# A two-layer RWKV and pooling trunk on one core: the row pitch of the FFN's input and the place of the residual's scalings

## The reference

```python
x = _layer_norm(ALPHA * x + h, ln_g[i, 0], ln_b[i, 0])
h = x @ w_in
gate, up = h[..., :D_FF], h[..., D_FF:]
x = _layer_norm(ALPHA * x + (jax.nn.silu(gate) * up) @ w_down, ln_g[i, 1], ln_b[i, 1])
```

## Time and profile before

| | |
|---|---|
| median of 3 runs | 2718.19 us (2717.26 to 2719.93) |
| profiled execution, its own time | 2718.26 us |
| its span, first to last instruction | 2716.7 us |
| TensorE matmuls, busy share of the span | 96% |
| VectorE, ScalarE, GpSimd | 64%, 43%, 5% |
| mean granted clock of TensorE, share of full speed | 0.982 |

### The profile page before, as it was taken

One profiled execution on the slowest core, in us unless ns is written; L12 is line 12 of the kernel. 1 busy time (PEld: TensorE's weight loads), 2 busy tenths in 40 slices (PEclk: granted clock), 3 DMA queues, 4 the chain that ended last, 5 costly groups with the idle time before them and its releaser, 6 DMA issues.

```text
span 2716.7 us, 56956 instructions
## 1 busy us (share of the span) xinstructions
PE 2595.1 (96%) x23305; PEld 2494.3 (92%) x23305; DVE 1744.5 (64%) x2764; ACT 1160.1 (43%) x1782; POOL 140.6 (5%) x211
## 2 busy tenths in 40 slices
PE   7979999999998899999999999878999999999997
PEld 7978888888788899999999999878999999999997
DVE  7877888888857655654455554686556444655546
ACT  5565555555534433333333333444333333333334
POOL 0000111111101000000000000100000000000000
PEclk9989999999999999999999999989999999999999
DMA  7622222222346556546665556524555556555553
GB/s 212 180 81 74 76 83 77 83 83 83 100 113 194 144 155 169 161 139 169 183 167 157 162 140 169 164 82 124 156 163 157 149 163 188 162 162 157 145 163 96
DMA packets 707053, 379.35 MB, mean 140 GB/s; under 512 B 16023, under 2 KB 699191, under 8 KB 706711
## 3 DMA queue, kind: packets, MB, share of 16 engines
q1 hardware_dynamic: 701040, 363.46, 47.8%
q0 software_dynamic: 5792, 13.34, 1.8%
q10 hardware_dynamic: 70, 0.39, 0.1%
HBM read 367.31 MB, written 10.62 MB: 139 GB/s over the span
## 4 chain that ended last, share of the span: by engine, by line
PE 80%; DVE 12%; ACT 4%; issue 2%; DMA 1%; DVEq 0%; SPq 0%; ACTq 0%
PE PS L741 24%; PE PS L742 23%; PE PS L743 23%; PE PS L894 3%; DVE WL L1739 3%; ACT WH L1270 2%; DVE PL L1856 1%; DVE ML L1754 1%; DVE TM L1747 1%; PE PS L926 1%; PE PS L1013 1%; PE PS L963 0%; PE PS L968 0%; PE PS L931 0%; DVE X L2214 0%
## 5 line engine op out<-in xcount | busy, mean ns | idle before, releaser
L1739 DVE TENSOR_TENSOR WL<-RAW,WH 128x2048 fp32r<-128x2048 f32 (+1 forms) x325 | 658.9, 2028 | 604.4 <-ACT WH L1270 604.3
L741 PE MATMUL PS<-UH,WH 128*128 128x290 f32 x2784 | 832.1, 299 | 17.0 <-DVE WL L1739 16.4
L1270 ACT ACTIVATE WH<-RAW 128x2048 fp32r<-128x2048 f32 (+1 forms) x325 | 552.0, 1699 | 648.1 <-PE PS L743 644.7
L743 PE MATMUL PS<-UH,WL 128*128 128x290 f32 x2784 | 827.2, 297 | 0.0
L742 PE MATMUL PS<-UL,WH 128*128 128x290 f32 x2784 | 824.7, 296 | 0.0
L741 PEld LDWEIGHTS PS<-UH,WH 128*128 128x128 f32 x2784 | 527.3, 189 | 18.9 <-issue 18.8
L742 PEld LDWEIGHTS PS<-UL,WH 128*128 128x128 f32 x2784 | 530.0, 190 | 0.1
L743 PEld LDWEIGHTS PS<-UH,WL 128*128 128x128 f32 x2784 | 525.7, 189 | 0.0
L741 PE MATMUL PS<-HH,WH 128*128 128x288 f32 x1408 | 413.9, 294 | 3.3 <-DVE WL L1739 3.3
L742 PE MATMUL PS<-HL,WH 128*128 128x288 f32 x1408 | 415.3, 295 | 0.0
L743 PE MATMUL PS<-HH,WL 128*128 128x288 f32 x1408 | 415.0, 295 | 0.0
(11 more groups left out here) (328 smaller groups left out, 3483.8 us busy)
## 6 DMA issues: line engine op xcount, KB each, us to landing
RAW<-in_ffn_w_in SPq DMA_DIRECT2D x176, 1024.0 KB, 5.7
RAW<-in_ffn_w_down SPq DMA_DIRECT2D x128, 704.0 KB, 4.8
RAW<-in_rw_wr SPq DMA_DIRECT2D x16, 1024.0 KB, 6.7
PR<-in_rw_wk SPq DMA_DIRECT2D x64, 256.0 KB, 3.0
PR<-in_rw_wv SPq DMA_DIRECT2D x64, 256.0 KB, 2.9
PR<-in_rw_wo SPq DMA_DIRECT2D x64, 256.0 KB, 3.2
S0N<-in_state_wkv POOLq DMA_DIRECT2D x64, 64.0 KB, 2.3
out<-SOS POOLq DMA_DIRECT2D x64, 64.0 KB, 2.7
```

The lines of the kernel that those rows point to most:

```text
L741: pe.matmul(out, wh, xh, start=first, stop=False)
L743: return pe.matmul(out, wl, xh, start=False, stop=last)
L1270: act.activation(WH[0:rows, j % 2, 0:n], RAW[0:rows, j, 0:n], ACT.Copy).then_inc(hi_ready, 1)
L1739: dve.tensor_tensor(WL[0:rows, j % 2, 0:n], RAW[0:rows, j, 0:n], WH[0:rows, j % 2, 0:n].bitcast(F32), ALU.subtract).then_inc(lo_ready, 1)
```

## The change

UH and UL get rows of 320 columns, 1280 bytes apart, of which 290 are used. They take 40,960 bytes up to the start of MH1: from the region's start UH is at 97,728 and UL at 118,208, both multiples of 64 and 64 more than multiples of 256. For it, ML0 follows MH0 without the 128 bytes between, and SUM and C12 move to XPS, NLN and GATE to LHH, LIN behind DP. UL's block c is kept in row (c + 2) mod 16. With these places 10 blocks, not 12, are free while the last units run (EARLY_IN). `gains_lo` writes in two pieces where its blocks go round the end. `scaled` and `normed` take a start block and do 4 blocks; they are called after each of the first four hidden units of a layer, for which the second call of `up` is written out too.

```diff
+EARLY_IN = 10
...
-        ML[0] = at("ML0", [P, KC, T], F32R, after("MH0") + 128)
+        ML[0] = at("ML0", [P, KC, T], F32R, after("MH0"))
...
-        UH = at("UH", [P, KC, T + 2], F32R, place["MH0"][0] - 128)
-        UL = at("UL", [P, KC, T + 2], F32R, place["ML0"][0] - 128)
...
+        UH = at("UH", [P, KC, 320], F32R, place["MH1"][0] - 2 * KC * 1280)
+        UL = at("UL", [P, KC, 320], F32R, after("UH"))
+        SUM = at("SUM", [P, T], F32, place["XPS"][0])
...
+        def ul(c):
+
+            return (c + 2) % KC
...
-                                     UH[:, k, :], UL[:, k, :], k == 0, k == KC - 1)
+                                     UH[:, k, 0:T + 2], UL[:, ul(k), 0:T + 2], k == 0, k == KC - 1)
...
-                        if kind == "late" and m < 12:
+                        if kind == "late" and m < EARLY_IN:
...
-            gains_hi(0, 12, KC)
-            for c in range(12, KC):
+            gains_hi(0, EARLY_IN, KC)
+            for c in range(EARLY_IN, KC):
                 input_hi(0, c)
...
+                for a, b in ((a, min(b, KC - 2)), (KC - 2, b)):
+                    for at, col in ((T, PCOL["ln_g"]), (T + 1, PCOL["ln_b"])):
+                        if a < b:
+                            dve.tensor_tensor(UL[:, ul(a):ul(a) + b - a, at:at + 1],
...
-            def scaled(k):
-
-                with dve.Fori(0, KC) as c:
+            def scaled(k, c0):
+
+                with dve.Fori(c0, c0 + 4) as c:
...
+                                if g == 0 and isinstance(i, int) and i < 2:
+                                    scaled(2 * layer, 4 * hc)
 
                     if g == 0:
                         up(0, False)
-                        scaled(2 * layer)
-                    with dve.Fori(1 - g, HG // 2 - 1) as i:
+                        up(1, False)
+                    with dve.Fori(0 if g else 2, HG // 2 - 1) as i:
                         up(i, False)
```

More of the change, by code:

```diff
@@ L189, in build @@
         OP = at("OP", [P, KC, T], F32, place["MH1"][0])
-        UH = at("UH", [P, KC, T + 2], F32R, place["MH0"][0] - 128)
-        UL = at("UL", [P, KC, T + 2], F32R, place["ML0"][0] - 128)
[L192 to L197, removed]
+        UH = at("UH", [P, KC, 320], F32R, place["MH1"][0] - 2 * KC * 1280)
+        UL = at("UL", [P, KC, 320], F32R, after("UH"))
+        SUM = at("SUM", [P, T], F32, place["XPS"][0])
+        C12 = at("C12", [P, 2, 4], F32, after("SUM"))
+        assert after("C12") <= after("XPS")
+        NLN = at("NLN", [P, 2, T], F32, place["LHH"][0])
+        GATE = at("GATE", [P, 2, T], F32, after("NLN"))
+        assert after("GATE") <= place["UH"][0]
         XROW = at("XROW", [P, 4, 3, 512], F32, place["MH1"][0])
@@ L263, in build @@
         DP = at("DP", [P, KC, T], F32, after("CI"))
+        LIN = at("LIN", [P, 2, T], F32, after("DP"))
+        assert after("LIN") <= after("XX")
         W3H = at("W3H", [P, 2048], F32R, place["DP"][0])
@@ L272, in build @@
         PS = [ctx.enter_context(nc.psum_tensor(f"PS{i}", [P, 512], F32)) for i in range(8)]
-        SUM = at("SUM", [P, T], F32, place["LHH"][0])
         IDN = CP[:, 0:P]
@@ L1512, in input_hi @@
             def input_hi(k, c):
-                act.wait_ge(out_free, 4 + OUT["o" if k == 0 else "pool"] + (c if c < 12 else KC - 1) + 1)
+                act.wait_ge(out_free, 4 + OUT["o" if k == 0 else "pool"] + (c if c < EARLY_IN else KC - 1) + 1)
                 act.activation(UH[:, c, 0:T], X[:, c, 1:T + 1], ACT.Copy, scale=par("ln_g", k * KC + c))\
@@ L1571, in layer_norm, with normed @@
                 act.activation(LNS[:, 0, :], LNS[:, 0, :], ACT.Sqrt).then_inc(ln["sd"], 1)
-            def normed(k):
-                with act.Fori(0, KC) as c:
+            def normed(k, c0):
+                with act.Fori(c0, c0 + 4) as c:
                     act.wait_ge(ln["scaled"], k // 2 * KC + c + 1)
@@ L1603, in up @@
                                                ACT.Copy).then_inc(hh_ready, 1)
+                                if g == 0 and isinstance(i, int) and i < 2:
+                                    normed(2 * layer, 4 * hc)
                     if g == 0:
                         up(0, False)
-                        normed(2 * layer)
-                    with act.Fori(1 - g, HG // 2 - 1) as i:
+                        up(1, False)
+                    with act.Fori(0 if g else 2, HG // 2 - 1) as i:
                         up(i, False)
@@ L2080, in gains_lo @@
             def gains_lo(k, a, b):
-                for at, col in ((T, PCOL["ln_g"]), (T + 1, PCOL["ln_b"])):
-                    dve.tensor_tensor(UL[:, a:b, at:at + 1], PAR[:, col + k * KC + a:col + k * KC + b].unsqueeze(2),
-                                      UH[:, a:b, at:at + 1].bitcast(F32), ALU.subtract)
+                for a, b in ((a, min(b, KC - 2)), (KC - 2, b)):
+                    for at, col in ((T, PCOL["ln_g"]), (T + 1, PCOL["ln_b"])):
+                        if a < b:
+                            dve.tensor_tensor(UL[:, ul(a):ul(a) + b - a, at:at + 1],
+                                              PAR[:, col + k * KC + a:col + k * KC + b].unsqueeze(2),
+                                              UH[:, a:b, at:at + 1].bitcast(F32), ALU.subtract)
             def input_lo(k, c):
                 dve.wait_ge(ln["hi"], HALVED[k] + c + 1)
-                dve.scalar_tensor_tensor(out=UL[:, c, 0:T], in0=X[:, c, 1:T + 1], scalar=par("ln_g", k * KC + c),
+                dve.scalar_tensor_tensor(out=UL[:, ul(c), 0:T], in0=X[:, c, 1:T + 1], scalar=par("ln_g", k * KC + c),
                                          in1=UH[:, c, 0:T].bitcast(F32), op0=ALU.mult, op1=ALU.subtract)\
@@ L2148, in _ @@
                 pass
-            dve.wait_ge(ln["hi"], 13)
-            gains_lo(0, 12, KC)
-            for c in range(12, KC):
+            dve.wait_ge(ln["hi"], EARLY_IN + 1)
+            gains_lo(0, EARLY_IN, KC)
+            for c in range(EARLY_IN, KC):
                 input_lo(0, c)
```

8 lines of the change are left out of this document (4 added, 4 removed).

## The result

The changed kernel takes 2728.56 us (median of 12 runs, 2721.55 to 2731.59), the kernel before, run beside it, 2720.29 us (12 runs, 2717.26 to 2725.01). The ratio is 1.0028, 95% interval 1.0019 to 1.0037: slower, where 2702.7 us were forecast. The profiled execution took 2731.59 us with a span of 2730.0 us, 13.3 us more than that of before.

The account below looks back on a forecast made before the run. TensorE's stream was taken to bound the kernel. Gains of 9.4 (pitch), 5.8 (scalings) and 0.3 us (early blocks), in sum 15.5, were subtracted from 2718.2 to give 2702.7 us, with a range from 2691 to 2713.

Parts of the forecast that it names:

- What bounds the kernel: Whole kernel: four fifths of the span lie on TensorE, so a microsecond off its stream is one off the time.
- Pitch of 1280 bytes: Up projections: rows all starting on multiples of 64 take 400 ns a triple, 3.3 ns less for 2816 triples, 9.4 us gained.
- the poor end: Up projections: worst outcome allowed for the new row spacing, no gain or a loss; the good end was 18 us.
- third rival: Up projections: rows starting alike within 256 bytes collide, 410 ns a triple, 18.9 us more, 2731.0 us; chance 0.07.
- The first rival: Up projections: the pitch brings nothing, as each row's last line stays half-filled; 2711.5 us, chance 0.20.
- Scalings four by four: After each layer norm: waits of 6.1 us a layer instead of 10.5, less 2.9 for lower clock; 5.8 us gained in both.
- the first wait: Before slab 4: TensorE starts 3.2 us later, then 3.4 us at half clock, which loses 1.5 us.
- The second wait: Before slab 8: TensorE starts 2.3 us later, with nothing charged for lower clock.
- late code: Second pair of slabs, written out instead of looped: its code could come late with nothing to hide it; nothing charged.
- The third predicted wait: Before slabs 6 and 10: TensorE waits 0.3 us at each.
- Ten early blocks: Two blocks fewer ahead of the last outputs: 0.5 us earlier in layer 0, 0.2 later in layer 1, together 0.3 gained.
- rivals 2 and 4: All rows at HH's pace, 2694.1 us, chance 0.19; clock gives back all of the scalings' gain, 2708.5 us, chance 0.07.

## Why the prediction was wrong, step by step

**What bounds the kernel** held: TensorE's chain, and a microsecond on its stream is one on the time.

**Pitch of 1280 bytes: the step that failed.** It was "The nearest rows are blocks 0 and 8: 0.40 us a triple, 133.3 ns a matmul. I take 400 ns". Measured were 3 times 136.0, 408 ns: 13.2 us lost instead of 9.4 gained. The two aligned blocks stood in a slab of 16 different starts, and what a matmul takes there tells little of a slab in which every row starts alike. The view that was read could have told: in the same slab block 14, which starts 48 off a multiple of 64, goes quicker still, 0.39 us, and blocks 3, 5, 6, 10, 11 and 12, none of them aligned, take 0.40 as well.

```profile
972.38 0.29 PE L741 MATMUL PS<-UH,WH 128*128 128x290 f32 x1
972.77 0.30 PE L741 MATMUL PS<-UH,WH 128*128 128x290 f32 x1
```

And the view shows steps of 0.01 us, where 3.3 ns were at stake. In the changed kernel, all of whose rows start alike, successive triples show 0.41 and 0.40 too:

```profile
1017.16 0.30 PE L747 MATMUL PS<-UH,WH 128*128 128x290 f32 x1
...
1017.57 0.30 PE L747 MATMUL PS<-UH,WH 128*128 128x290 f32 x1
...
1017.97 0.30 PE L747 MATMUL PS<-UH,WH 128*128 128x290 f32 x1
```

So 0.40 and 0.41 could not tell an aligned row from another. A stretch as a whole settles into a pace, and one place has more than one: 136.0 and 133.3 in the kernel with rows 64 lower, and in the changed kernel itself, where layer 1's slabs 4 and 5 go at 133.3 and the slabs from 6 on, behind an interruption of 0.1 us, at 136.0. The forecast's pace exists and even occurs from aligned rows; to take it for the only one was the error. Rows of 1160 bytes, whose starts are mixed, give 134.4 in every half, between the two.

The layout was also bounded too narrowly: the poor end was set to "nothing, or a loss", and only the third rival carried the loss. Its size was nearly right (410 ns a triple, 2731.0 us), the point from which it decides (405.5 ns) was passed, and slabs of 6.53 us are over its mark of 6.49. That is luck: its mechanism isn't supported, for rows parted within 256 bytes still take 135.6 ns, and rows at 48, which lie a multiple of 256 apart as well, take 133.3. The first rival's half-filled last line has for it at most that without the two columns which begin it the pace is 2.7 ns lower, where 0.8 are proportional; against it, rows that begin 48 bytes later reach into as many lines, whether of 16 or of 64 bytes, and go as those of 288 columns.

The Trainium skill, page "SBUF — State Buffer", section "Specifications (TRN2)", speaks of lines of 16 bytes; by it, as an estimate, 1160 bytes from 0, 8, 24, 32 or 48 touch 73 lines each and should go alike. The trace doesn't agree: they went at 133.3 to 136.7 ns, so the lines do not tell the places apart.

**Scalings four by four: right in kind, half in size.** Forecast were 12.2 us of waits and 3.0 of lower clock in both layers, instead of 21.0. Starts less 48 matmuls of 136.0 ns give waits of 3.4 and 3.4 us in layer 0, 3.4 and 2.2 in layer 1, with 0.1 ahead of slab 6 there: 12.5. Lower clock cost 2.6 + 1.6 + 1.6 = 5.8. The gain is 2.7 instead of 5.8, and the kernel with this part alone gained 2.6 by its medians, not clear of noise. The mis-sized term is the clock: the first wait was charged with 1.5 us and the second "with nothing", but the second was followed by 0.50 in both layers, and the first cost 2.6 us in layer 0 (1.6 in the kernel with this part alone) and nothing in layer 1. The second wait of layer 0 was also a microsecond longer than the 2.3 worked out: "nothing is charged" for late code, but the third group of scalings lost 0.96 us to issue. This group runs in a call that is now written out, but so does the fourth, and layer 1 loses nothing; the gap comes in both kernels that have this part, and its cause stays open. The third predicted wait, 0.3 us before slabs 6 and 10, did not come in layer 0.

**Ten early blocks: right.** 0.5 us earlier in layer 0 were taken; the idle time before the last outputs fell by 1.54 us and that before the variance products grew from 0.26 to 1.11: 0.7 gained. In layer 1, charged with 0.2, these two waits grew by 0.1 together (2.25 to 2.27 and 1.10 to 1.17).

**The chances.** The pace's two sides were known from one trace in which neither layout to come was to be seen, yet 0.85 was given to faster. The forecast, its rivals 2 and 4 and most of the range all rested on the one reading of blocks 0 and 8.

What stays open is what lies beneath the paces: which of TensorE's reads or loads meet each other, and why 48 bytes do better than 0. The runs show that columns, row start and pitch all count, that the weights' place or the 64 bytes that moved with it does, and that a pace mostly lasts until TensorE's stream is interrupted; what picks it at the next start was not found. The turned order of UL's rows and the new places of the smaller buffers came with every run of the new layout and were not tried by themselves.

## What to carry to other kernels

Don't take the pace of a layout from single instructions inside another layout; count matmuls over a long stretch, in each stage by itself, and give a new layout a range with both signs until one run has shown it. Before a loop is cut into smaller waits, look for idle time on its own engine that takes the whole of it: here three of four waits of 2 to 3.3 us were followed by half clock, and four scalings in VectorE's wait for ScalarE cost nothing. When a layout change disappoints, try the start of the rows before giving up the pitch.

## What was not expected

- One layout has two paces at full clock, 136.0 and 133.3 ns (rows 64 lower), each kept through a whole stretch of 130 us.
- 34 columns less made a matmul 18 to 23 ns quicker than 136.0, and 14.2 would be the columns at 2.4 GHz. The Trainium skill, page "TensorE: Matmul & The Clock Gate", section "Wait — 56ns, not 53.3ns?", gives the columns at 2.4 GHz and some 2.5 ns for bfloat16; an estimate by it is 123.3 ns for 290 columns and 109.2 for 256. The stretches here show more, 132.8 to 136.7 and 113.3 to 117.9.
- 2.02 us idle were followed by a clock of 0.50 (layer 1, slab 8), 3.25 us by 1.00 (layer 1, slab 4): the length of the wait alone does not tell.
